# Turning the first expert pass's rows by one-hot products on strided residual columns, with the slot-table products moved inside the first gate product

## The reference

```python
xl = xl + gt1_l * rms_norm(mix_l, g_post_mix[layer])
hl = rms_norm(xl, g_pre_ffn[layer]) * (1.0 + sc2_l) + sh2_l
# hier_moe(hl): 4 groups x 8 experts, top-1 group, top-2 experts in it
yb = (silu(xr @ w_gate[e]) * (xr @ w_up[e])) @ w_down[e]     # xr: the rows routed to expert e
```

## Time and profile before

| | |
|---|---|
| median of 3 runs | 1854.52 us (1852.51 to 1858.04) |
| the profiled execution's own time | 1858.59 us |
| its span in the trace | 1856.8 us |
| busy share of the span: PE, DVE, ACT, POOL | 93%, 48%, 26%, 26% |
| mean granted TensorE clock | 0.974 of full speed |

### The profile page before, as it was taken

The page is one execution under the profiler, slowest core; times in us unless marked ns, Lnnn a source line. Parts: engine busy times, 40 slices in busy tenths (PEclk is TensorE's granted clock), DMA queues, the critical chain, the costliest instruction groups (busy, mean ns, idle before and its releaser), DMA issues.

```text
span 1856.8 us, 19778 instructions
## 1 busy us (share of the span) xinstructions
PE 1730.3 (93%) x7344; PEld 1060.8 (57%) x7344; DVE 891.0 (48%) x1428; ACT 487.9 (26%) x839; POOL 477.4 (26%) x516
## 2 busy tenths in 40 slices
PE   5999999999997999999999999999898887988877
PEld 2555555555546878887885578885533332333332
DVE  3626455465456787777876687663330000000004
ACT  3221422414233434445444100002321101111012
POOL 1214042140446557665564000000010000010000
PEclk9999999999998999999999999999899989999999
DMA  7221323312320111111114344467779999999995
GB/s 303 95 79 57 114 68 97 121 55 68 103 68 23 46 46 50 40 34 56 45 39 143 125 136 136 139 225 259 287 308 429 429 429 430 429 385 429 429 425 236
DMA packets 153985, 344.35 MB, mean 185 GB/s; under 512 B 15462, under 2 KB 105791, under 8 KB 140858
## 3 DMA queue, kind: packets, MB, share of 16 engines
q1 hardware_dynamic: 136048, 319.45, 45.3%
q10 hardware_dynamic: 13114, 15.89, 2.6%
q0 software_dynamic: 4752, 8.05, 1.1%
HBM read 333.54 MB, written 19.09 MB: 190 GB/s over the span
## 4 chain that ended last, share of the span: by engine, by line
PE 81%; DMA 7%; DVE 6%; issue 3%; ACT 1%; DVEq 0%; SPq 0%; ACTq 0%
PE bank L943 12%; PE bank L2934 10%; PE bank L2056 10%; PE bank L586 9%; PE bank L984 6%; PE bank L2952 6%; DMA arena<-in_w_up_dram 5%; PE bank L2098 3%; PE bank L614 3%; PE bank L1591 2%; PE bank L536 2%; PE bank L558 2%; PE bank L1028 2%; PE bank L1036 1%; PE bank L1573 1%
## 5 line engine op out<-in xcount | busy, mean ns | idle before, releaser
L943 PE MATMUL bank<-stay,arena 128*128 128x512 f32 (+1 forms) x704 | 240.0, 497 | 0.0
L2934 PE MATMUL bank<-arena 128*64 128x512 f32 x832 | 186.8, 606 | 15.3 <-DMA arena<-in_w_up_dram 8.8
L943 PEld LDWEIGHTS bank<-stay,arena 128*128 128x128 f32 x704 | 132.4, 190 | 99.7 <-issue 92.3
L2934 PEld LDWEIGHTS bank<-arena 128*64 128x64 f32 x832 | 66.0, 140 | 131.4 <-issue 116.5
L2952 PE MATMUL bank<-arena 128*64 128x512 f32 x416 | 110.7, 693 | 32.3 <-issue 15.8
L1461 POOL TENSOR_TENSOR arena<-arena 128x256 f32<-128x256 f32 x112 | 85.2, 761 | 192.2 <-DVE arena L1727 124.8
L3075 DVE TENSOR_TENSOR arena<-arena,bank 128x512 f32<-128x512 f32 x17 | 11.7, 688 | 234.4 <-PE bank L2934 234.4
L984 PE MATMUL bank<-arena,stay 128*128 128x512 f32 x256 | 114.6, 595 | 3.9 <-DVE arena L1236 3.9
L2806 POOL DMA_INDIRECT y_dram<-arena x16 | 16.1, 1008 | 380.9 <-DVE arena L3082 380.3
L2056 PE MATMUL bank<-stay,arena 128*128 128x256 f32 x456 | 103.1, 379 | 0.0
L3081 DVE COPY arena<-bank 128x512 f32<-128x512 f32 x16 | 11.1, 692 | 191.2 <-PE bank L2952 191.2
(11 more groups left out here) (492 smaller groups left out, 3016.8 us busy)
## 6 DMA issues: line engine op xcount, KB each, us to landing
arena<-in_w_gate_dram SPq DMA_DIRECT2D x24, 2048.0 KB, 18.8
arena<-in_w_down_dram SPq DMA_DIRECT2D x24, 2048.0 KB, 23.1
arena<-in_w_up_dram SPq DMA_DIRECT2D x22, 2048.0 KB, 23.3
arena<-in_w_in_dram SPq DMA_DIRECT2D x58, 512.0 KB, 3.9
arena<-in_w_ada_dram SPq DMA_DIRECT2D x12, 2048.0 KB, 10.8
stay<-in_w_gate_dram SPq DMA_DIRECT2D x8, 2048.0 KB, 22.6
stay<-in_w_up_dram SPq DMA_DIRECT2D x8, 2048.0 KB, 18.3
arena<-in_w_in_dram ACTq DMA_DIRECT2D x6, 2048.0 KB, 9.7
```

What stands on the lines that cost most here:

```text
L943: mm = pe.matmul(ps[:, 0:n], w[:, k, :], hT[:, k, o:o + n], start=(k == 0), stop=(k == KT - 1))
L2934: mm = pe.matmul(b[cols, :], xgT[r][:, k, cols], w[u][:, k, :], start=(k == 0), stop=(k == KT - 1))
```

## The change

The turned rows of the first pass are produced directly. For each k the residual's columns `c*8 + k` are the stationary operand, read with a step of 8 elements, and `hot` is the moving one, 128 columns wide, so that the product is already turned. The two ScalarE copies and the eight transposes go. The four first tiles signal `FIRST_HALF`, on which the first four column operations now wait. The slot-table products are no longer in `route_tensor`: `slot_table` is called inside the first gate product, between k = 3 and k = 4.

```diff
-            act.wait_ge(s_rp, FIRST_HALF)
-            act.copy(xg[0][:, 0:512], bank[0][:, :])
-            act.wait_ge(s_rp, FIRST_GATHERED)
-            act.copy(xg[0][:, 512:1024], bank[1][:, :]).then_inc(s_ra, 1)
...
             pe.wait_ge(s_rv, FIRST_ROWS)
-            for hf in range(2):
+            for k in range(KT):
                 for cc in range(LCH):
-                    mm = pe.matmul(bank[hf][:, :], hot[:, cc, :, :].rearrange("p e s -> p (e s)"), xl[:, cc, hf * 512:(hf + 1) * 512],
-                                   start=(cc == 0), stop=(cc == LCH - 1))
-                mm.then_inc(s_rp, 1)
-            pe.wait_ge(s_ra, FIRST_STORED)
-            x = xg[0].rearrange("p (c k) -> p k c", k=KT)
-            for k in range(KT):
-                mm = pe.transpose(bank[k // 4][:, (k % 4) * P:(k % 4 + 1) * P], x[:, k, :], ident[:, :])
+                    mm = pe.matmul(bank[k // 4][:, (k % 4) * P:(k % 4 + 1) * P], xl[:, cc, :].rearrange("p (c k) -> p k c", k=KT)[:, k, :],
+                                   hot[:, cc, :, :].rearrange("p e s -> p (e s)"), start=(cc == 0), stop=(cc == LCH - 1))
+                if k == KT // 2 - 1:
+                    mm.then_inc(s_rp, 1)
             mm.then_inc(s_xgt, 1)
+
+        def slot_table(pe):
             pe.wait_ge(s_iota, ROWS_NUMBERED)
             pe.wait_ge(s_rv, SLOT_CHOICES)
             for j in range(NT):
...
             def columns(done, r, early=False):
-                act.wait_ge(s_xgt, done + 1)
+                if not early:
+                    act.wait_ge(s_xgt, done + 1)
                 for k in range(KT):
+                    if early and k == 0:
+                        act.wait_ge(s_rp, FIRST_HALF)
+                    if early and k == KT // 2:
+                        act.wait_ge(s_xgt, done + 1)
...
                 for k in range(KT):
                     if first and k == KT // 2:
+                        slot_table(pe)
                         pe.wait_ge(s_xgc, 1)
```

More of the change, by code:

```diff
@@ L251, in build @@
         s_ra = sem("routing_and_output_scalar_stages")
-        GROUP_EXPS, EXPERT_EXPS, FIRST_STORED, FIRST_COLUMNS, OUTPUT_RSTD = 1, 2, 3, 4, 5
+        GROUP_EXPS, EXPERT_EXPS, FIRST_COLUMNS, OUTPUT_RSTD = 1, 2, 3, 4
         s_rp = sem("routing_tensor_stages")
-        LOGITS, FIRST_RANKS, COUNTS, RANKS, FIRST_HALF, FIRST_GATHERED, SLOT_TABLE = 1, 2, 3, 4, 5, 6, 7
+        LOGITS, FIRST_RANKS, COUNTS, RANKS, FIRST_HALF, SLOT_TABLE = 1, 2, 3, 4, 5, 6
         s_wdt = sem("w_dt_loaded")
```

## The result

The changed kernel takes 1860.18 us (median of 20 runs, 1856.51 to 1864.44), the kernel before 1854.7 on the same chip (20 runs). The ratio is 1.0027, 95% interval 1.0019 to 1.0034: 5.0 us slower, 3.5 to 6.3. I had forecast 1.6 us faster, with 1858.9 as the end of the range.

A forecast was written before the change was run, and what follows sets the result against it. The expert stage was taken as bound by the weight stream, which starts at the first gate product's end: 2.7 us earlier less 1.1 for the table gives 1.6, so 1854.5 - 1.6 = 1852.9 us; range 1849.5 to 1858.9.

The forecast's parts named there:

- the small hole: Weight-stream dip at 1385 to 1390, where the next load waits for the first down product; forecast to stay as large.
- I take 0.12, as the strided row runs: Direct one-hot products: 0.12 us for each of 64 records, near bounds 0.112 and 0.159, taken from strided transposes.
- rival of the dear load: Strided weight loads in the one-hot block are slow: 5.0 us slower, 1859.5 at the far bound; chance 0.08.
- far bound of 0.224 per record: One-hot products if the strided load doubles the record time: block with clock and table 17.3 us.
- 1.9 us for half speed: Start of the one-hot block: 3.7 us at 1.2 GHz lose about 1.9 us, the same in both kernels.
- more than the sum: Rival: clock fall misses the down product, small hole closes, about 1 us; 3.1 us gained in all, 1851.4; chance 0.11.
- covered: First-pass gathers, issued 2.4 us later, still land in 3.6 to 5 us, before their rows are needed at 1369.4.
- The three things that hang on the table: Behind the 2.4 us later slot table: Silu short by 0.2 us, gathers covered, list of experts costing nothing.
- the hole of the stream: Ten microseconds of almost no weight transfer, ending with the first gate product; the first two gathers were expected in it.
- The first half of the tiles as cover for the column operations: One-hot block: first tiles done by about 1350.7, four column operations by 1352.3, hidden before the gate product at 1354.4.
- the table's 1.1 us ahead of the gate product's end: Slot table inside the first gate product adds 1.1 us, cutting the 2.7 us gain at its end to 1.6.
- the late gather: Rival: first gather falls behind the weight chunk, takes 14.8 us, TensorE waits; end 4.4 us later, 1858.9; chance 0.07.

The follow-up runs named there:

- table_first: The changed kernel with the slot-table products back ahead of the first gate product: 1859.24 us, ratio 1.0013 to the kernel before.
- packed_stationary: The changed kernel with 128 adjacent columns as stationary operand, so its rows hold wrong columns: 1854.74 us, ratio 0.9987 to the kernel before.
- table_moved_alone: The kernel before with only the slot table moved inside the first gate product: 1860.13 us, ratio 1.0019.
- gathers_late: The kernel before with GpSimd's first two gathers waiting for the list of experts, not the tables; slot table stays early: 1861.68 us, ratio 1.0029.
- packed_copy_table_first: The changed kernel reading a packed residual copy by ScalarE, first copy written early, slot table ahead of the gate product: 1854.61 us, ratio 0.9988 to the kernel before.
- table_moved_again: The kernel before with only the slot table moved inside the first gate product, measured a second time: 1860.5 us, ratio 1.0019.
- before_look: The kernel before, unchanged, traced once more: 1856.03 us in one run.
- steps: The changed kernel with stationary-operand steps of 1, 2, 3, 4, 6, 8, 16 and 32 elements, one per tile, wrong columns: 1856.95 us in one run.
- strided_moving: The changed kernel with operands exchanged, `hot` stationary and the strided residual moving, so the product is unturned: 1860.0 us in one run.
- the packed copies' pair: Changed kernel reading packed residual copies, first copy early: slot table inside the gate product 1855.91 us (0.9997), ahead of it 1854.61 us (0.9988).

## Why the prediction was wrong

**An account by the stream.** The end follows the weight stream, so I counted for each trace when the stream starts, and how much of it is missing behind that (in windows of 10 us from the start: the bytes short of 430 GB/s, divided by 430 GB/s). Microseconds against the profiled kernel before:

```
                         start  missing by +30  missing by +400   start + missing   measured ratio
before                      0        2.9              8.3                0                1
changed                  +4.0        1.6              9.3             +4.9          +5.0 (1.0027)
table_first              +4.0        1.7              7.0             +2.6          +2.4 (1.0013)
packed_stationary        -2.9        1.7              9.2             -2.0          -2.4 (0.9987)
table_moved_alone        +0.6        1.7              9.7             +1.9          +3.5 (1.0019)
gathers_late             -0.5        7.7             14.3             +5.4          +5.4 (1.0029)
packed_copy_table_first  -2.8        1.7              7.0             -4.1          -2.2 (0.9988)
```

Five of the six agree to 1.6 us or better, packed_copy_table_first to 1.9; why it agrees less stays open. The account and the ratio come from different executions, and one trace isn't exact to better than about a microsecond: from the logits the output's stores begin at 513.48 and 514.50 in the two traces of the changed kernel, at 509.62 and 508.87 in those of the kernel before. The changed kernel's 5.0 us are thus three terms: 4.0 from the start, -1.3 at the small hole, +2.3 at a later one.

**Term 1, the block: the step that failed.** "I take 0.12, as the strided row runs" was the wrong price. The record interval is 15.20 / 64 = 0.2375 us. I had taken it from transposes, whose load rose only from 141 to 188 ns with a step of 8. A true float32 product's load rises from 190 to 336 ns, and packed_stationary shows that nothing but the step does it. Both signs that I had named for this, loads of 240 ns or more and a block above 11 us, came true. This is my rival of the dear load; I had given it 0.08, and its far bound of 0.224 per record was even a little short. A second part of the step failed the other way: I added 1.9 us for half speed, but the strided interval is nearly the same at 0.50 and at 1.00 of the clock (11 records in 2.46 us, 22 in 5 us), so this block loses next to nothing there, where the packed one does (8.53 us against 64 x 0.112 = 7.2).

**Term 2, the small hole: what "more than the sum" said of the clock came true beside it.** The down product runs at full clock (7.09 us against 8.78), the load behind it comes 18.65 us after the stream's start where it was 20.34, and the missing part by +30 us falls from 2.9 to 1.6. I had priced it at about 1 us (I let a load begin about 1 us behind its issue; behind the stream's start 1.5 to 1.8 us are missing in every trace). It is 1.3, and all kernels of the table have it but the one with late gathers. It isn't a property of the new products: table_moved_alone has the old block and gains it too, table_moved_again, the same kernel, doesn't (21.6 us between the two loads, not 18.65). The traces show the clock (a mean of 0.66 from 1375 to 1380 before, 1.00 in the changed kernel); what decides it they don't show.

**Term 3, the late table: "covered" was wrong.** The three things that hang on the table went as I said: the list of experts made nobody wait, the Silu's cover is used up and short by 0.17 us (I had said 0.2), the rows of pass 1 are there in time. What I left out is that the gathers' own transfer must go somewhere. In the kernel before it lay in the hole of the stream. Now the first gather is issued 1.9 us ahead of the weights and the second 0.35 us behind them, so that they share the weights' time. I had called both the quick ones; the second takes 10.5 to 11.1 us to land in all ten traces with a late table, and 3.5 to 3.6 in the four with early table and gathers. Where it shows is 137 us later, when TensorE waits for up weights again. Changed kernel (stream's start 1363.93), TensorE in order of time:

```profile
1501.38 9.95 PE L2934 MATMUL bank<-arena 128*64 128x512 f32 x32 [3.35 <-DMA arena<-in_w_up_dram]
...
1578.03 8.78 PE L2952 MATMUL bank<-stay,arena 128*64 128x512 f32 x32 [2.98 <-ACT arena L2848]
```

and the same with the table first (stream's start 1367.82):

```profile
1504.25 8.68 PE L2934 MATMUL bank<-arena 128*64 128x512 f32 x32 [2.41 <-DMA arena<-in_w_up_dram]
...
1581.05 7.09 PE L2952 MATMUL bank<-stay,arena 128*64 128x512 f32 x32 [2.98 <-ACT arena L2849]
```

Counted from the stream's start, the first product begins at 137.45 against 136.43: its weights land 1.0 us later. The second begins at 214.10 against 213.23, 0.9 later, and takes 1.7 us more, since it runs in part at half clock (mean granted clock 0.66 in its first 5 us, against 1.00). 2.6 us in all. The load that hangs on it is issued at 223.07 against 220.51, and the lag stays through the step with two passes on one set of weights, where the stream runs dry. Windows there, changed kernel:

```profile
1630.00:1635.00 5.00, 5.00 (x18) 1.90 (x16) 0.00 (x0) 0.00 (x0) 0.00 (x0) 0.66 0.52 211
1635.00:1640.00 5.00, 5.00 (x26) 2.02 (x24) 1.29 (x2) 0.00 (x0) 0.37 (x1) 1.00 0.45 104
1640.00:1645.00 5.00, 5.00 (x26) 1.95 (x24) 0.00 (x0) 0.53 (x1) 1.66 (x2) 1.00 0.90 383
```

and with the table first:

```profile
1630.00:1635.00 5.00, 4.97 (x16) 1.96 (x18) 0.00 (x0) 0.00 (x0) 0.00 (x0) 0.66 0.87 365
1635.00:1640.00 5.00, 5.00 (x26) 2.00 (x24) 1.15 (x2) 0.00 (x0) 0.00 (x0) 1.00 0.45 173
1640.00:1645.00 5.00, 5.00 (x26) 1.98 (x24) 0.14 (x1) 0.00 (x0) 2.04 (x2) 1.00 0.97 347
```

The first three windows carry 187 GB/s more in sum with the table first, 5 x 187 / 430 = 2.2 us of stream. Over all traces, the stream that is missing from 260 to 290 us behind its start:

| | us missing |
|---|---|
| table and gathers early (before, before_look, table_first, packed_copy_table_first) | 4.5 to 4.7 |
| table late, down product quick at the small hole (seven traces, the changed kernel's two among them) | 6.8 to 7.4 |
| table late, down product slow there (steps, strided_moving, table_moved_again) | 4.6, 5.9, 6.3 |
| table early, gathers late (gathers_late) | 6.3 |

That the late table costs is shown clear of noise by table_moved_alone, twice (at least 1.7 us, with a start 0.6 to 0.8 later), and narrowly by changed against table_first; the medians of the packed copies' pair lean the same way, and its traces show it. That it costs through a later landing and one more slow product is what the two traces above, and the pair of packed copies with the same two differences (138.18 against 136.50, 8.79 us against 7.09, the load at 223.50 against 220.60), show. That it is the gathers that make the landing late, and not something else that hangs on the table, is argued: gathers_late, with the table early, has the larger hole too, but its late rows also moved everything behind them. Why the landing is a whole microsecond later stays open: the bytes moved in the last 10 us ahead of the stream differ by only 16 to 18 GB/s, 0.4 us of stream. Two of the kernels with a late table (steps, strided_moving) kept the slow product at the small hole and reached the output's stores 1.9 and 2.5 us sooner behind it than the changed kernel did; so the later price depends on the rhythm of waits and clock as well as on the table.

**What was right.** The question asked, whether the stream starts earlier: its start, moved by 6.9 us between two kernels, moved the end by 6.8. The first half of the tiles as cover for the column operations, the table's 1.1 us ahead of the gate product's end (0.9), no wait for gathered rows.

**The range and the chances.** With the block at 15.3, my own sum gives 15.3 + 1.1 - 12.3 = 4.1 us slower, 1858.6, just inside the range; the measured 1860.18 lies 1.3 us above its end of 1858.9. The dear load was one of my rivals, at 5.0 us slower or 1859.5, and the range, which I let run to the late gather, ended short of it. That its total came so near the measured 5.0 us is in part luck: it counted 1.9 us for the clock that this block doesn't lose, and nothing for the late table.

## What to carry to other kernels

Price an operand's step from an instruction of the same kind and type; where the trace has only another kind, the far bound is a real case and belongs in the range. Here a step of 4 float32 or more on the stationary operand, or of 8 on the moving one, doubled the time of a 128-column product; packing first on an idle engine won most of it back. In a stage bound by a stream of transfers, ask of everything that is moved into the stream's time what it takes from the stream, and not only whether its own reader waits: a gather or a small table belongs in the hole.

## What the runs showed of the hardware beyond the expected

- Reading float32 with a step by TensorE: 0.112 us per 128 columns packed, 0.175 at step 3, 0.22 to 0.24 at steps 4 to 32, for a stationary operand; 15.19 us for 64 records at step 8 for a moving one. At step 2 the few loads at full clock took 196 ns, near the packed 192. The interval at step 8 is nearly the same at granted clocks of 0.50 and 1.00.
- Transposes hide most of it: a load at step 8 took 188 ns and eight ran at 0.12 us each, in the same kernel in which products at step 8 took 0.2375.
- ScalarE's read at step 8 took 2.08 us per 1024 columns, 1.15 packed.
- A gather issued 0.64 us ahead of 4 MB of weights landed after 11.8 us (gathers_late). Issued 1.9 us or more ahead, the gathers of passes 1 and 2 landed after 3.5 to 5.3 us; issued 0.35 us behind, after 10.5 to 11.1.
